# Hybrid decoder layer on one core: seven pairs of gate feature rows computed as Strassen products over 320 and 320 tokens

## The reference, cut to what matters

```python
qa, ka, va, qr, kr, vr, gr, gate_a, gate_b = jnp.split(xn @ w_in, splits, axis=-1)
...
r = rms_plain(orr).reshape(B, T, RET_V_W) * jax.nn.silu(gr)
m = jax.nn.sigmoid(gate_a + ba) * (a @ w_pa) + jax.nn.sigmoid(gate_b + bb) * (r @ w_pb)
return m @ w_o
```

## Time and profile before

| what | value |
|---|---|
| median of the runs | 2741.04 us |
| the profiled execution's own time | 2738.75 us |
| its span | 2737.0 us |
| granted TensorE clock | 0.999 |
| gates stage | 1010 to 1597 us |
| TensorE busy | 99% of the span |
| VectorE, ScalarE, GpSimd busy | 50%, 27%, 32% |

### The profile page before, as it was taken

How to read it: one execution, slowest core, us unless ns; L and a number is a source line. 1 busy time by engine, 2 the same in 40 slices (tenths; PEclk the granted TensorE clock), 3 DMA queues, 4 the chain that set the end, 5 groups by cost and what they waited for, 6 DMA issues and landing times.

```text
span 2737.0 us, 41596 instructions
## 1 busy us (share of the span) xinstructions
PE 2706.9 (99%) x16114; PEld 2334.2 (85%) x16114; DVE 1368.7 (50%) x2728; ACT 740.8 (27%) x1549; POOL 868.0 (32%) x697
## 2 busy tenths in 40 slices
PE   8999999999999999999999999999999999999998
PEld 6888877777777779888888899999899999998887
DVE  6431355547666655666555533243485555542224
ACT  5111122225555542222222221011332222221012
POOL 2533423302211232221122235354124444455230
PEclk9999999999999999999999999999999999999999
DMA  4323356553333334456554554334122222245221
GB/s 161 113 100 132 107 195 205 196 178 116 99 130 108 106 130 163 160 192 198 188 190 149 191 188 145 126 120 159 47 83 71 76 91 72 72 149 175 87 61 66
DMA packets 277923, 362.14 MB, mean 132 GB/s; under 512 B 28530, under 2 KB 172530, under 8 KB 277746
## 3 DMA queue, kind: packets, MB, share of 16 engines
q1 hardware_dynamic: 277746, 359.74, 39.5%
HBM read 257.24 MB, written 111.35 MB: 135 GB/s over the span
## 4 chain that ended last, share of the span: by engine, by line
PE 95%; DVE 3%; ACT 1%; issue 1%; DMA 0%; POOL 0%; SPq 0%; DVEq 0%; ACTq 0%; POOLq 0%
PE psum L538 24%; PE psum L1334 14%; PE psum L2747 14%; PE psum L2073 12%; PE psum L563 10%; PE psum L1024 3%; PE psum L1046 2%; PE psum L2729 2%; PE psum L2122 2%; PE psum L2106 1%; PE psum L2771 1%; PE psum L1448 1%; PE psum L1036 1%; PE psum L2115 1%; PE psum L1000 1%
## 5 line engine op out<-in xcount | busy, mean ns | idle before, releaser
L364 POOL TENSOR_TENSOR w_h<-stage,ones 128x512 fp32r<-128x512 f32 x268 | 305.6, 1168 | 1297.8 <-PE psum L2073 384.2
L371 POOL TENSOR_TENSOR w_l<-stage,w_h 128x512 fp32r<-128x512 f32 x268 | 359.1, 1367 | 123.3 <-DVE acc L1174 118.6
L538 PE MATMUL psum<-w_h,xt_h 128*128 128x512 f32 x864 | 343.6, 398 | 3.5 <-POOL w_l L385 2.8
L538 PE MATMUL psum<-w_h,xt_l 128*128 128x512 f32 x864 | 341.8, 396 | 0.0
L538 PE MATMUL psum<-w_l,xt_h 128*128 128x512 f32 x864 | 341.8, 396 | 0.0
L2073 PE MATMUL psum<-xt_h,w_h 128*128 128x384 f32 x744 | 263.7, 354 | 0.1
L2073 PE MATMUL psum<-xt_h,w_l 128*128 128x384 f32 x744 | 244.4, 328 | 0.0
L2073 PE MATMUL psum<-xt_l,w_h 128*128 128x384 f32 x744 | 244.3, 328 | 0.0
L416 POOL TENSOR_TENSOR w_l<-stage,w_h 128x512 fp32r<-128x512 f32 x106 | 139.4, 1315 | 268.8 <-ACT w_h L2841 268.8
L1334 PE MATMUL psum<-w_h,xt_h 128*128 128x512 f32 x512 | 219.3, 428 | 0.0
L1334 PE MATMUL psum<-w_l,xt_h 128*128 128x512 f32 x512 | 202.4, 395 | 0.0
(11 more groups left out here) (307 smaller groups left out, 5719.2 us busy)
## 6 DMA issues: line engine op xcount, KB each, us to landing
stage<-in_w_in_dram SPq DMA_DIRECT2D x88, 512.0 KB, 5.6
proj<-edge SPq DMA_DIRECT2D x112, 256.0 KB, 2.1
stage<-in_w_gu_dram SPq DMA_DIRECT2D x88, 256.0 KB, 3.8
out_dram<-acc SPq DMA_DIRECT2D x43, 512.0 KB, 3.7
acc<-proj SPq DMA_DIRECT2D x82, 256.0 KB, 3.1
gates<-edge SPq DMA_DIRECT2D x32, 544.0 KB, 3.4
acc<-in_cache_k_dram SPq DMA_DIRECT2D x32, 512.0 KB, 5.3
acc<-in_cache_v_dram SPq DMA_DIRECT2D x32, 512.0 KB, 4.6
```

Of the source, the lines that this page charges most:

```text
L364: last = nc.gpsimd.tensor_tensor(w_h[s][:, a:b, :], src, one.unsqueeze(1).to_broadcast([128, b - a, WN]), ALU.mult)
L371: last = nc.gpsimd.tensor_tensor(w_l[s][:, a:b, :], stage[h][:, a - lo:b - lo, :], w_h[s][:, a:b, :].bitcast(F), ALU.subtract)
L538: last = nc.tensor.matmul(psum[:, bank, :], x, w[s][:, k, :], start=k == 0 and n == 0, stop=k == nk - 1 and n == len(passes) - 1)
```

## The change

The 32 rows are taken as 16 pairs p of 48 steps y. Pairs 0 to 7 and 15 stay plain, pairs 8 to 14 (`GATE_FAST`) become *fast*. In a fast pair the tokens 0 to 639 are two halves of 320, the features two rows, the depth two halves of 512, and seven products (P1 to P7, each 4 k blocks x 3 matmuls of 320 columns) take the place of eight; the last 448 tokens stay plain (`PLAIN0`, `PLAIN1`, 8 k blocks x 3 matmuls each). Each of the nine is a unit in the two alternating banks.

- **Weights.** Loads are by pair (`load_gate_pair`, two DMAs of 512 KB, half a `stage` buffer each). High parts are made by ScalarE (`gate_high`), low parts by GpSimd (`gate_low`), in five slots. In fast pairs GpSimd also makes four weight sums (S1 to S4).
- **Activations.** The sums T1 to T4 are made in pairs 0 to 3 by VectorE (`tg_sum_made` at y = 5, 8 adds; `tg_low_made` at y = 34) and ScalarE (4 copies at y = 20).
- **Results.** ScalarE copies each product from PSUM, VectorE makes seven adds of 320 columns at later steps, and ScalarE applies the sigmoids.
- **`w_pa`.** `W_PA` is loaded in pair 15 and split by ScalarE and GpSimd; `W_PA + 1` is loaded and split after the stage.

```diff
+GATE_FAST = range(GATE_PAIRS // 2, GATE_PAIRS - 1)
+P1, PLAIN0, P2, PLAIN1, P6, P7, P4, P5, P3 = range(9)
...
+    def load_gate_pair(sp, p):
+        if p < 2:
+            sp.wait_ge(w_split, split_count(W_FM - 1, 1))
+        else:
+            sp.wait_ge(op_split, gate_op(p - 1))
+        src = w_in[0].rearrange("(k p) n -> p k n", p=128)
+        for h in range(2):
+            sp.dma_start(stage[h][:, :, 256 * (p % 2):256 * (p % 2 + 1)],
+                         src[:, 4 * h:4 * h + 4, W_FM * WN + 256 * p:W_FM * WN + 256 * (p + 1)]).then_inc(
+                             stage_loaded[p % 2], 16)
...
+                for name in ("A11", "A12", "A21"):
+                    gate_low(p, name)
+                gate_sum_made(p, "S3")
+                gate_low(p, "A22")
+                for name in ("S2", "S1", "S4"):
+                    gate_sum_made(p, name)
+                for name in GATE_OPS[False][4:]:
+                    gate_low(p, name)
...
+    def gate_high(act, p, name):
+        o = gate_op(p, name)
+        if name[0] == "S":
+            act.wait_ge(sums_ready, gate_sum(p, name))
+        else:
+            act.wait_ge(stage_loaded[p % 2], 32 * (W_FM + p // 2 + 1))
+        nc.scalar.copy(gop_h(o), gate_source(p, name)).then_inc(op_high, 1)
```

SyncE's steps:

```diff
+                    if gate_plain(p) and y == 29:
+                        store_gate(2 * p)
+                    if p and gate_plain(p - 1) and y == 5:
+                        store_gate(2 * p - 1)
+                    if p and not gate_plain(p - 1) and y == 4:
+                        store_gate(2 * p - 1)
+                    if p and not gate_plain(p - 1) and y == 8:
+                        store_gate(2 * p - 2)
+                    if 1 <= p < GATE_PAIRS - 1 and y == 6:
+                        load_gate_pair(sp, p + 1)
+                    if p == GATE_PAIRS - 1 and y == 6:
+                        load_w(sp, W_PA)
```

TensorE, a product of a fast pair:

```diff
+                    for k in range(4):
...
+                        for n, (wt, low) in enumerate(((gop_h, False), (gop_h, True), (gop_l, False))):
+                            last = nc.tensor.matmul(psum[:, gate_bank(idx), 0:GH], wt(o)[:, k, :], gate_x(moving, k, low),
+                                                    start=k == 0 and n == 0, stop=k == 3 and n == 2)
```

ScalarE, plain pairs:

```diff
+            if y and y % 8 == 0 and (p < GATE_PAIRS - 1 or y <= 24):
+                plain_unit(p, y // 8 - 1)
+            if p < GATE_PAIRS - 1:
+                if y == 1:
+                    gate_high(act, p + 1, "A11")
+                if y == 25:
+                    gate_high(act, p + 1, "A12")
+                if y == 26:
+                    gate_high(act, p + 1, "A21")
```

More of the change, by code:

```diff
@@ L115, in v_step @@
 def v_step(n, name):
[L117 removed]
+    return len(BY_DVE) + N_GATE_STEPS + sum(len(v_names(m)) for m in range(n)) + v_names(n).index(name) + 1
 def s_step(n, name):
@@ L408, in gpsimd_program @@
+        for n, k in enumerate(PA_ORDER):
+            pool.wait_ge(op_high, N_GATE_OPS + n + 1)
+            last = nc.gpsimd.tensor_tensor(w_l[0][:, k, :], stage[k // 4][:, k % 4, :], w_h[0][:, k, :].bitcast(F),
+                                           ALU.subtract)
+            if n >= KD - 2:
+                last.then_inc(w_split, 1)
+        pool.wait_ge(gate_full, N_GATE_UNITS)
+        split(W_PA + 1, 1, no=tile_no(W_PA + 1), loaded=32 * (W_PA + 1))
         for w in range(W_PB, W_GU):
-            split(w, w % 2, used=banks_before(w - 1))
+            split(w, w % 2, used=banks_before(w - 1), no=tile_no(w), loaded=32 * w)
@@ L543, in pe_token_tile, with pe_feature_tile @@
                     behind(t)
-    def pe_feature_tile(pe, xh, xl, s, split, g, order=range(4), free=None, ready=None, beside=None):
+    def pe_feature_tile(pe, xh, xl, s, split, g, order=range(4), free=None, ready=None, beside=None, holder=None):
         for j, m in enumerate(order):
@@ L2078, in gate_groups, with wait_bank @@
-            yield from last_row()
+            for p in range(GATE_PAIRS - 1):
+                if gate_plain(p):
+                    for r in range(2):
+                        yield from plain_row(p, r)
+                else:
+                    yield from fast_pair(p)
+            yield from plain_row(GATE_PAIRS - 1, 0)
+            yield from last_row()
+        def wait_bank(idx):
+            if idx == 0:
+                pe.wait_ge(out_read, STEPS)
+            elif idx == 1:
+                pe.wait_ge(x_read, len(X_ORDER) - 1)
+            else:
+                pe.wait_ge(gate_read, idx - 1)
@@ new lines, in wide_group @@
+        def wide_group(p, r, k, idx, a, width):
+            o = gate_op(p, (("A11", "A12"), ("A21", "A22"))[r][k // 4])
+            if k % 4 == 0:
+                pe.wait_ge(op_split, o + 1)
+            for n, (wt, x) in enumerate(((gop_h, xt_h1), (gop_h, xt_l1), (gop_l, xt_h1))):
+                last = nc.tensor.matmul(psum[:, gate_bank(idx), 0:width], wt(o)[:, k % 4, :], x[:, k, a:a + width],
+                                        start=k == 0 and n == 0, stop=k == KD - 1 and n == 2)
+            if k == KD - 1:
+                last.then_inc(gate_full, 1)
@@ new lines, in plain_steps @@
+        def plain_steps(p, y):
+            if y and y % 8 == 0 and (p < GATE_PAIRS - 1 or y <= 24):
+                plain_unit(p, y // 8 - 1)
+            if p < GATE_PAIRS - 1:
+                if y == 1:
+                    gate_high(act, p + 1, "A11")
+                if y == 25:
+                    gate_high(act, p + 1, "A12")
+                if y == 26:
+                    gate_high(act, p + 1, "A21")
+            if p in T_PAIRS and y == T_HIGH_MARK:
+                act.wait_ge(t_step, 3 * p + 1)
+                for t in range(1, 5):
+                    last = nc.scalar.copy(tg_piece(t, p, False), tg_sums(t, p))
+                last.then_inc(t_step, 1)
+            if p == GATE_PAIRS - 1 and y in PA_MARKS:
+                merge_high(PA_MARKS[y])
```

431 lines of the change are left out of this document (329 added, 102 removed).

## The result

The changed kernel takes **2808.89 us** (median of 5 runs, 2805.93 to 2812.91) against 2741.04 (five runs, 2739.61 to 2742.42): ratio 1.0246, interval 1.0235 to 1.0256, or 67.9 us slower. The forecast was 2737.6 in a range of 2728 to 2752.

A forecast was written before the change was run, and what follows sets the result against it. TensorE, busy for 99% of the span, was taken as the bound. Terms -12.7 + 7.6 + 0.5 + 0.5 + 0.7 + 1.0 - 1.0 = -3.4 us gave 2735.4 profiled, 2737.6 as median, range 2728 to 2752.

The forecast's parts named there:

- the late load: Plain pairs: ScalarE stands at y = 1 until the next pair's weights land, delaying the recurrence; 7.6 us.
- the fast pairs: Engines other than TensorE in pairs 8 to 14: mostly hidden, small terms for S2, stores and VectorE slowed by GpSimd.
- 1.0 taken back: Plain pairs: four GpSimd pieces a pair instead of eight, so 1.0 of 3.0 us of TensorE waits is won.
- The matmul gain: TensorE in seven fast pairs: fewer columns save 1.81 us a pair, 12.7 us in all.
- Rival D: Fast pairs: 448 columns priced like 512, gain only 3.4 us, about 2747 us; chance 0.05.
- S2: GpSimd's weight sum, wanted by ScalarE at y = 2 of fast pairs: waits 0.6 to 3 us each, costing 0.5.
- GpSimd beside VectorE: Fast pairs: GpSimd's bursts slow VectorE's operations; 1.0 us, from 0 to 5.
- the store at y = 8: Row store moved behind two loads on SyncE, needed landed at y = 14: 0.5 us for all, 0.7 in pair 15.
- The rest costs nothing: After the gates stage, splitting `W_PA + 1` is hidden behind the merge's first tile, 48 us; no cost.
- Rival C: Fast pairs: GpSimd holds up ScalarE at S2 (y = 2), stalling TensorE; 14 us more, 2751 us; chance 0.27.

The follow-up runs named there:

- a11_late: The changed kernel with ScalarE's first high part of the next pair's weights made at y = 25 of a plain pair instead of y = 1: 2775.43 us.
- no_fast: The changed kernel with all 16 pairs plain, no T sums, and the next pair's first high part at y = 25: 2747.92 us.
- loads_early_s2_late: loads_early with the high part of S2 at y = 8 instead of y = 2 in the fast pairs: 2767.35 us.
- gp_small: loads_early with every GpSimd piece of the fast pairs cut to 32 of 512 columns, the rest left out: 2753.24 us.
- loads_early: The changed kernel with loads of pairs 2 to 15 issued at y = 36 two pairs ahead, not y = 6 of the pair before: 2766.54 us.

## Why the prediction was wrong

The direction was wrong: -3.4 us forecast, +67.9 measured. The runs split the 67.9 into 33.3 for the late load (7.6 in the forecast), 27.5 for the fast pairs with the sums T, columns included (-12.7 + 0.5 + 0.5 + 0.7 + 1.0 = -10.0 in the forecast), and 7.1 for the new order of loads and splits (nothing, and 1.0 taken back). So two terms failed by their size, and the clock was in none.

- **The matmul gain** (-12.7): right; 448 columns cost 0.204 us. Rival D falls.
- **The late load** (7.6) is the largest step that failed: the mechanism and its place were right (the longest stall in pair 7), its size wrong by three to four times: 25.1 us by itself, 33.3 in the changed kernel. Three things in that step failed. First the landing: I took 4.5 us, "between the minimum and the middle", because there were only two loads; the median was 6.1, and ScalarE went on 8.2 us behind the store's start in pair 1. The middle of the earlier trace rows had been the better estimate. With it the sum had a bound of 13.6. Second, even so the waits came to 16.3 (13.7 + 2.6), more than that bound: for pairs 1, 2, 3, 6 and 7 I had 0.1, 0.6, 1.5, 1.1 and 4.3, and the trace has 2.6, 2.2, 3.6, 2.0 and 5.9. Third, I priced a wait at its own length, though some are followed by a stretch at 1.2 GHz.
- **The clock** was in no term. I read 1.00 in each stretch of the kernel before and took it as given. In its gates stage the longest wait was 1.8 us, so no row of that stage showed what a wait of 3 to 6 us does. One place in that trace held a warning. After TensorE's first wait, 8.2 us at the start, matmuls of 512 columns start 0.43 us apart up to 15 us, about twice the 0.2315 of the earlier trace rows, and 0.23 from 18 us on:

```profile
14.23 0.63 PE L538 MATMUL psum<-w_l,xt_h 128*128 128x512 f32 x1
14.66 0.63 PE L538 MATMUL psum<-w_h,xt_h 128*128 128x512 f32 x1
```

(The granted clock is given as 1.00 there, so only the distances tell it.) The bound from both sides that I gave to the unknown prices was missing here, and the range was too narrow by this alone.
- **The fast pairs** (0.5 for S2, 0.5 and 0.7 for stores, 1.0 for VectorE, from 0 to 5): the sum was wrong by an order. Seven of them, with the sums T, cost 34.6 - 7.1 = 27.5 us net of the 12.7 they save (a11_late against no_fast). S2 was harmless (loads_early_s2_late). The 1.0 for GpSimd beside VectorE should have been some 13 (gp_small, which takes away all that GpSimd's full pieces do, to ScalarE too). I had read the 1.45 us of the earlier trace rows as the price of one add; it can be the price of every operation of that kind, and the root has several in a row in the chain that TensorE waits for. The place of the loads cost 8.9 (loads_early against a11_late), through `values_high`, which was in no step, and through the store at y = 8: priced at 0.5 for all pairs, it had one wait of 4.5 us.
- **"The rest costs nothing"**: TensorE waited 3.1 us for `W_PA + 1` at the merge; it does so in no_fast too, as part of its 7.1.
- **S2** idles ScalarE by 16.7 us as worked out (0.6 to 3 a pair forecast, 2.4 measured), at no cost. **Rival C** had the right sign and named GpSimd, and had the wrong victim: VectorE's chain was held up, not ScalarE at S2. That its 14 us lie beside the 13.5 of gp_small is luck.

Open is what the fast pairs cost besides. gp_small is 5.1 us slower than no_fast, with 12.7 us of columns saved, which leaves some 18 us. In it TensorE still waits 5.5 us for VectorE beside the four full-size pieces of pair 15, and ScalarE's reads (L2427, L2425, L2443) account for 8.3 us of waits. No run took ScalarE's added work, its waits for stores or the sums T away alone.

## What to carry to other kernels

Where one engine is busy for 99% of the time at its upper clock, a new wait can cost more than its length: removed work returns 1.8 us a pair here, and a new wait of 2 to 6 us takes its own length and in most cases a stretch at half speed. So count the new waits first, and take for a landing at least the middle of the rows. In these runs work moved to GpSimd was not free for VectorE: look for short operations with two SBUF inputs in the chain that the bound engine waits for.

## What the runs showed of the hardware that I had not expected

- A single short wait in the middle of dense work can put TensorE at its lower level: 0.27 us for 320 columns after a wait of 2.61 us (1043.27), 0.32 for 384 some 2 us after one of 1.59 (1108.92), against 0.147 and 0.176. After waits of 2.24 (1074.91) and 2.54 us (1371.92) it stayed at the upper one, so the length of the wait alone doesn't decide. Between 1100 and 1130, with waits of 1.59, 3.61 and 3.08 us, the granted clock was 0.68:

```profile
1100.00:1130.00 30.00, 21.73 (x92) 16.96 (x91) 17.48 (x37) 4.93 (x11) 2.55 (x2) 0.68 0.33 107
```

- VectorE operations of 128 x 1 elements with two inputs in SBUF can last as long as what is left of GpSimd's piece: 1.25 us in place of 0.16. Making an operation smaller doesn't prevent it (adds of 32 columns: up to 1.33 us, half of them 0.19 or less). Giving it an operand in PSUM does: 0.222 us on average, and L2604 with one input in PSUM stays between 0.157 and 0.160 us in loads_early.
